# Attention outputs by features: values stationary on two column halves, probabilities moving and divided before they are transposed

## What is computed

```python
p_cmp = jnp.where(vis, jax.nn.softmax(s, axis=-1), 0.0)
o_cmp = jnp.einsum('bgrsc,bcgd->bsgrd', p_cmp.astype(vc.dtype), vc)
...
o = (g[:, :, 0] * o_cmp.astype(jnp.float32) + g[:, :, 1] * o_slc.astype(jnp.float32)
     + g[:, :, 2] * o_win.astype(jnp.float32))
...
m = jnp.maximum(jnp.max(s, axis=-1, keepdims=True), sk)
e = jnp.exp(s - m)
p = e / (jnp.sum(e, axis=-1, keepdims=True) + jnp.exp(sk - m))
o = jnp.einsum('bngrqk,bnkgd->bnqgrd', p.astype(vb.dtype), vb)
...
merged = jax.nn.sigmoid(ga) * (o_a @ w_branch_a[i]) + jax.nn.sigmoid(gb) * (o_b @ w_branch_b[i])
...
x = x + jnp.concatenate([o_a, o_b, o_c], axis=-1) @ w_out[l]
```

## Time and profile before

| | |
|---|---|
| device time, median of 3 runs | 1260.78 us (1260.34 to 1265.6) |
| device time of the profiled execution | 1260.99 us |
| its span | 1259.2 us |
| PE busy | 1228.6 us (98%) |
| DVE busy | 791.7 us (63%) |
| ACT busy | 609.6 us (48%) |
| GpSimd busy | 66.4 us (5%) |
| granted TensorE clock, mean | 0.997 |

### The profile page before, as it was taken

How to read it: one execution, slowest core, us unless ns; L and a number is a source line. 1 busy time by engine, 2 the same in 40 slices (tenths; PEclk the granted TensorE clock), 3 DMA queues, 4 the chain that set the end, 5 groups by cost and what they waited for, 6 DMA issues and landing times. The chain is left out here.

```text
span 1259.2 us, 21554 instructions
## 1 busy us (share of the span) xinstructions
PE 1228.6 (98%) x8764; PEld 1131.6 (90%) x8764; DVE 791.7 (63%) x1095; ACT 609.6 (48%) x831; POOL 66.4 (5%) x58
## 2 busy tenths in 40 slices
PE   8999999999999999999999899999999989999997
PEld 7999999989998999999999789999999978999996
DVE  4665556657866655555799655555458977654554
ACT  5444345355536443435755554444465464544343
POOL 0000000200000000000530000000004200000000
PEclk9999999999999999999999999999999999999999
DMA  9576565455335565556465056655644734566550
GB/s 286 176 227 193 175 184 149 129 159 169 134 119 199 179 192 197 173 193 185 151 126 168 28 174 203 197 175 193 187 140 119 159 101 151 174 195 192 176 198 33
DMA packets 200915, 209.62 MB, mean 166 GB/s; under 512 B 58136, under 2 KB 177552, under 8 KB 200848
## 3 DMA queue, kind: packets, MB, share of 16 engines
q1 hardware_dynamic: 200400, 208.21, 53.8%
q10 hardware_dynamic: 448, 0.46, 0.2%
HBM read 207.61 MB, written 1.05 MB: 166 GB/s over the span
## 5 line engine op out<-in xcount | busy, mean ns | idle before, releaser
L1366 DVE TENSOR_TENSOR w_lo<-raw,w_hi 128x2048 fp32r<-128x2048 f32 (+2 forms) x192 | 432.9, 2258 | 270.5 <-ACT w_hi L1014 269.9
L1014 ACT ACTIVATE w_hi<-raw 128x2048 fp32r<-128x2048 f32 (+2 forms) x192 | 359.4, 1876 | 246.3 <-PE bank L1890 214.8
L1890 PE MATMUL bank<-n_hi,w_hi 128*128 128x256 f32 (+1 forms) x1600 | 455.4, 285 | 1.5 <-DVE w_lo L1366 1.5
L1890 PE MATMUL bank<-n_hi,w_lo 128*128 128x256 f32 (+1 forms) x1600 | 452.8, 283 | 0.0
L1890 PE MATMUL bank<-n_lo,w_hi 128*128 128x256 f32 (+1 forms) x1600 | 452.7, 283 | 0.0
L1890 PEld LDWEIGHTS bank<-n_hi,w_hi 128*128 128x128 f32 (+1 forms) x1600 | 305.3, 191 | 5.6 <-DVE w_lo L1366 1.7
L1890 PEld LDWEIGHTS bank<-n_lo,w_hi 128*128 128x128 f32 (+1 forms) x1600 | 305.3, 191 | 2.1 <-issue 0.2
L1890 PEld LDWEIGHTS bank<-n_hi,w_lo 128*128 128x128 f32 (+1 forms) x1600 | 305.3, 191 | 0.0
L1890 PE MATMUL bank<-w_hi,hid_hi 128*128 128x512 f32 x440 | 172.7, 392 | 1.3 <-DVE hid_lo L1439 1.1
L1890 PE MATMUL bank<-w_lo,hid_hi 128*128 128x512 f32 x440 | 171.8, 391 | 0.0
L1890 PE MATMUL bank<-w_hi,hid_lo 128*128 128x512 f32 x440 | 171.4, 389 | 0.0
(11 more groups left out here) (268 smaller groups left out, 1485.5 us busy)
## 6 DMA issues: line engine op xcount, KB each, us to landing
raw<-in_w_ff_dram SPq DMA_DIRECT2D x64, 1024.0 KB, 5.3
raw<-in_w_in_dram SPq DMA_DIRECT2D x31, 1024.0 KB, 5.4
raw<-in_ffn_down_dram SPq DMA_DIRECT2D x22, 1024.0 KB, 4.9
raw<-in_ffn_up_dram SPq DMA_DIRECT2D x21, 1024.0 KB, 5.4
raw<-in_ffn_gate_dram SPq DMA_DIRECT2D x20, 1024.0 KB, 5.4
raw<-in_w_out_dram SPq DMA_DIRECT2D x12, 1024.0 KB, 5.1
raw<-in_w_in_dram SPq DMA_DIRECT2D x12, 256.0 KB, 4.0
raw<-in_w_uq_dram SPq DMA_DIRECT2D x24, 128.0 KB, 4.0
```

Source lines behind the costliest of these rows:

```text
L1014: nc.scalar.activation(wh(s)[:, c0:n], raw[:, s % RING, c0:n], ACT.Copy).then_inc(hi_ready, 1)
L1366: V.tensor_tensor(wl(s)[:, c0:n], raw[:, s % RING, c0:n], wh(s)[:, c0:n].bitcast(f32), ALU.subtract).then_inc(lo_ready, 1)
L1890: mm = MM(out, stat(k, a), mov(k, b), start=(first and k == 0 and n == 0), stop=(last and k == K - 1 and n == 2), skip_group_check=True)
```

## The change

Values become stationary, 64 columns of them, and the transposed probabilities move: the upper group writes partitions 0 to 63 of the output bank, the lower group 64 to 127, so that the output stands by features. Where heads share their values, one product takes all heads of a group (N = 256 or 512). The compressed, selected and window branches are summed in one bank (`output_of`), so the coefficients, sums and gates, have to be in the probabilities ahead. A new step `n` does that between `s` and `t`: DVE works out `pcoef`, GpSimd multiplies the upper group's probabilities with it, DVE the lower group's. The step `o` then only splits the bank into `on_hi` (ACT) and `on_lo` (DVE). The steps `ot` are gone, `mixt` transposes the retention's output alone, swa comes first in the first block, the branch product takes swa's weights first, and in the second block `wout` begins with its second half between the last rounds. `probsT` gets two more buffers.

```diff
-    S += gate[1] + [("cmp1", "v"), ("rope", 0, "kc")] + scores[3] + weighted[1] + turned[2]
+    S += gate[1] + [("cmp1", "v"), ("rope", 0, "kc")] + scores[3] + normed[2] + weighted[1] + turned[2]
...
-    S += gate[7] + [("sigmoid",)] + weighted[7] + turned[8] + [("ot", "a", 1), ("ot", "b", 0)] + weighted[8]
-    S += [("ot", "b", 1), ("branch",)]
+    S += gate[7] + [("sigmoid",)] + normed[8] + weighted[7] + turned[8] + [("cv", 1)] + weighted[8] + [("o", 0, "nsa", 1), ("branch",)]
...
+        scores, normed, turned, weighted = in_rounds(l, [("dsa", 0), ("dsa", 1), ("mla", 0), ("mla", 1)])
+        S += scores[0] + scores[1] + [("ukv", l)] + normed[0] + turned[0] + scores[2] + [("ukvv", l)] + normed[1] + turned[1]
+        S += [("rety", l)] + scores[3] + weighted[0] + normed[2] + weighted[1] + [("mixt", l)] + turned[2] + scores[4] + normed[3]
+        S += [("wout", l, 0)] + turned[3] + weighted[2] + normed[4] + turned[4] + weighted[3] + weighted[4]
+        S += [("wout", l, n) for n in range(1, 4)]
...
+                if st[0] == "n" and st[4] % 2 == 0:
...
+                    pool.wait_ge(coef_ready, CO[(l, a, t, next(r for r in rounds(a, t) if g in r))] + 1)
+                    by = pcoef[:, RSLOT[a], t, hs].unsqueeze(2).to_broadcast([P, nh, nk])
+                    p = probs[:, q % 4, 0:nh * nk].rearrange("p (h k) -> p h k", h=nh)
+                    nc.gpsimd.tensor_tensor(p, p, by, ALU.mult).then_inc(normed[0], 1)
...
+                elif kind == "n":
+                    _, l, a, t, g = st
+                    r = next(r for r in rounds(a, t) if g in r)
+                    if g != r[0]:
...
+                        dve.wait_ge(coef_ready, CO[(l, a, t, r)] + 1)
...
+                        V.tensor_tensor(p, p, bc(by, len(heads), nk), ALU.mult).then_inc(normed[1], 1)
+                        continue
+                    dve.wait_ge(exp_done, ATT[(l, a, t, r[1])] + 1)
...
+                    ins = V.reciprocal(c, sums)
+                    if a in GATE:
+                        link(ins)
+                        dve.wait_ge(*free_count(("toks", 0)))
+                        ins = V.tensor_tensor(c, c, of(gates[:, t, 8 * GATE[a]:8 * GATE[a] + 8]), ALU.mult)
+                    ins.then_inc(coef_ready, 1)
...
+                elif kind == "o":
+                    ob, ks, tok = output_blocks(st)
+                    act.wait_ge(pv_done, ON[st[1:]][1])
...
+                    nc.scalar.activation(on_hi[:, ks, tok], ob, ACT.Copy).then_inc(ot_hi, 1)
...
-                    pe.wait_ge(exp_done, q + 1)
+                    pe.wait_ge(normed[st[4] % 2], NRM[st[1:]] + 1)
...
-                    for i, h in enumerate(heads):
-                        for blk in range(t + 1):
-                            c = (i * (t + 1) + blk) * P
-                            mm = MM(acc[o % 2][:, h * HD:h * HD + HD], probsT[:, n % 2, c:c + P], values(a, h, blk),
-                                    start=(blk == 0), stop=(blk == t))
...
+                    for blk in range(t + 1):
+                        for i in range(nh if a == "mla" else 1):
+                            for rows_, heads, pT in sides:
+                                c0, n = column_of(a, heads[i]), (1 if a == "mla" else nh)
+                                mm = MM(ob[rows_, c0:c0 + n * P].rearrange("p (i c) -> p i c", c=P), values(a, heads[i], blk), pT[:, i:i + n, blk, :],
+                                        start=(first and blk == 0 and i == 0), stop=(blk == t), skip_group_check=True)
```

More of the change, by code:

```diff
@@ L128, in schedule @@
           ("rope", 0, "nq0"), ("proj", 0, "vv"), ("rope", 0, "sk"), ("proj", 0, "sq0"), ("rope", 0, "k"),
-          ("xpe", "k"), ("proj", 0, "nq1"), ("rope", 0, "sq0"), ("xpe", "v"), ("cmp1", "k")]
-    scores, turned, weighted = in_rounds(0, [("slc", 1), ("slc", 0)] + [(a, t) for a in ("win", "swa") for t in range(NT)])
+          ("xpe", "k"), ("proj", 0, "sq1"), ("rope", 0, "sq0"), ("xpe", "v"), ("cmp1", "k")]
+    scores, normed, turned, weighted = in_rounds(0, [("swa", 1), ("swa", 0)] + [(a, t) for a in ("slc", "win") for t in range(NT)])
@@ L168, in schedule @@
     return S
+GATE = {"cmp": 0, "slc": 1, "win": 2}
 HEADS = {"slc": 8, "win": 8, "swa": 8, "dsa": 4, "mla": 8}
@@ L201, in outputs @@
     def outputs(job):
[L202 to L218, removed]
+        return [("pv", l) + job] + ([("o", l) + job[:2]] if job[2] == last[job[:2]] and job[0] not in GATE else [])
+    return ([[("s", l) + job for job in jobs] for jobs in turns], [[("n", l) + job for job in jobs] for jobs in turns],
+            [[("t", l) + job for job in jobs] for jobs in turns], [[st for job in jobs for st in outputs(job)] for jobs in turns])
 PROJ = {(0, "kcvc"): [(512, 256)], (0, "misc"): [(1816, 128), (1280, 24)], (0, "kk"): [(768, 128), (1024, 128)],
@@ L420, in job @@
                 _small[0] += 1
-            if b is None and key[0] == "t":
+            if b is None and key[0] in ("t", "mixt"):
                 b = 2 + _turned[0] % 2
@@ L742, in values, with turned_probs, column_of, output_blocks @@
             return vm[:, blk, 64 * h:64 * h + 64]
+        def turned_probs(n):
+            return probsT[:, n % 4, :] if n % 4 < 2 else probsT2[:, n % 4 - 2, :]
+        def column_of(a, h):
+            return P * (h % 4 if a in ("slc", "win") else h // 2)
+        def output_blocks(st):
+            n = 2 if st[2] == "dsa" else 4
+            k0 = {"nsa": 0, "swa": 4, "dsa": 4, "mla": 0}[st[2]]
+            ob = acc[ON[st[1:]][0] % 2][:, 0:n * P].rearrange("p (k c) -> p k c", k=n)
+            return ob, slice(k0, k0 + n), slice(st[3] * P, st[3] * P + P)
         def mask_of(a, t):
@@ L751, in two_blocks @@
         RSLOT = {"slc": 0, "win": 1, "swa": 2, "cmp": 3, "mla": 4, "dsa": 5}
-        GATE = {"cmp": 0, "slc": 1, "win": 2}
         def quarter(q):
@@ L1335, in _ @@
                 elif kind == "wout" and st[2] < 2:
-                    ahead(SL[st])
+                    ahead(SL[st], 1 if st[1] and st[2] == 0 else 2)
         @block.vector
@@ L2223, in _ @@
                     _, l, a, t, g = st
-                    heads, n, o = groups(a, t)[g], PVN[st[1:]], ON[st[1:4]][0]
+                    r = next(r for r in rounds(a, t) if g in r)
+                    if g != r[0]:
+                        continue
+                    key = output_of(l, a, t)
+                    ob, begun = acc[ON[key][0] % 2], key in opened
                     if g == 0:
@@ L2353, in _ @@
                                 mm = MM(pb[:, :], (on if l else xn)(4 * half + k, a)[:, t * P:t * P + P], w(s, b)[:, k * 512:k * 512 + 512],
[L2354 removed]
+                                        start=(not last and k == 0 and j == 0), stop=(last and k == 3 and j == 2),
                                         skip_group_check=True)
[L2356 removed]
+                        if last and t == 0:
                             mm.then_inc(filled(("wq", l, 2 * c)), 1)
```

307 lines of the change are left out of this document (144 added, 163 removed).

## The result

The changed kernel takes 1302.61 us (median of four, 1298.91 to 1303.44). Beside four runs of the kernel before (median 1263.19, 1260.34 to 1265.88) that is a ratio of 1.031, 95% interval 1.027 to 1.034. The runs of the kernel before fall in two groups, 1258 to 1262 us at a mean granted clock of 0.995 to 0.998 and 1263 to 1269 at 0.990 to 0.995; its profile is of the first group, and every ratio here takes both. The prediction was 1300, range 1275 to 1320. The profiled execution took 1303.44 us with a span of 1301.6, where before had 1260.99 and 1259.2: the span is 42.4 us longer.

A forecast was written before the change was run, and what follows sets the result against it. PE, busy 98% of the span, was taken to bound the kernel. From 1261 us, 55.9 us of new waits come and 27.1 us of work and waits go (+28.8), and the clock adds 10: 1300 us, range 1275 to 1320.

The forecast's parts named there:

- The bound: Whole kernel: PE, busy 98% of the span, sets the end; PE work removed is won, PE waiting is lost.
- PE work that goes: On PE: value products 6.9 us less in the first block, 7.0 in both layers; transposes 4.4 less.
- Old waits: PE's waits in attention of layers 1 and 2, 7.3 us, and in the branch products, 1.46, go.
- the fast rival of 1234 us: Division ready when PE's value products end, so no new waits: 1234 us; chance 0.03.
- The chain of the wait: Ahead of each round's transposes PE waits for score step, coefficients, GpSimd's product and hops, less cover: 55.9 us in all.
- the first wait: First block, first round (swa, t=1): wait for the division with a rotation of 0.96 as cover, 3.8 us.
- The terms for the layers: Layers 1 and 2: four waits for the division in each, 2.9, 1.8, 4.3 and 3.8 us, sum 12.8.
- The lock: DVE and GpSimd share a port pair, locked for a whole instruction; GpSimd's product taken as 1.9 us, shortest 1.29.
- The clock: After some PE waits the clock halves, costing 1.65 us a stretch; six of 17 counted: +10 us, from 0 to 28.
- The rival in which every wait lowers the clock: All 17 waits on PE bring a low clock stretch: 28 us instead of 10, 1318 us; chance 0.12.
- The sum: Whole kernel: 55.9 us come and 27.1 go, +28.8, with +10 for the clock: 1300 us.
- The break-even of 1.6 us a wait: Mean new wait of PE, over 17 waits, at which the 27.1 us that go would be used up.

The follow-up runs named there:

- the last order: Changed kernel with divisions moved ahead on DVE and GpSimd, and output copies and splits moved later in first block and layers: 1247.16 us, ratio 0.988.
- the other orders: Nine experiments keeping the changed kernel's 8628 instructions: PE busy 1211.8 to 1213.5 us, median 1212.4, with their low clock taken off.
- the early order: Changed kernel with each division moved ahead in DVE's and GpSimd's order, no instruction added or taken away: 1257.56 us, ratio 0.994.
- the filled run: Changed kernel, order kept, with unused products of 256 columns put on PE ahead of each wait for the division: 1283.19 us, ratio 1.015.
- thin products: Changed kernel, order kept, with the division's products cut to the first key of each head: 1270.79 us, ratio 1.005.

## Why the prediction came out, step by step

- **The bound.** PE decides: right. DVE had 4 us more to do after the change and GpSimd 27, and neither is near the span in its total (61% and 7%); the time is PE's work plus PE's waits in every run.
- **PE work that goes.** Right for the value products. Where no wait hides it, in the last order above, a round of the first block with them takes 1.01 us from their start to the next (1.07 taken), where it took 1.84:

```profile
293.33 1.08 PE L2250 MATMUL bank<-probsT,scr 128*64 128x512 f32 x4
294.34 1.09 PE L2223 MATMUL bank<-cst,probs 128*128 128x128 f32 x8
```

  That is two products of 512 columns, one on each half, in little more than the 0.96 that one takes, and four of 256 take as long. Column halves do run side by side. The sum was over-sized: -16.8 against -18.3 by the table, -14.5 by the other orders. The place of what is missing can be read. PE's busy time in layer 1 and the stretch up to layer 2, before the change and in the last order (columns as above):

```profile
658.50:990.20 331.70, 324.96 (x2268) 297.18 (x2267) 213.96 (x301) 165.59 (x231) 22.40 (x17) 1.00 0.53 159
```
```profile
651.40:979.30 327.90, 321.45 (x2245) 291.55 (x2244) 215.44 (x306) 163.71 (x229) 29.48 (x22) 1.00 0.53 161
```

  It is 3.5 us less, and 3.6 from there to the end, where 3.5 + 1.3 = 4.8 was counted for each layer. The first block has some 8.2 of its 8.7. Which operation of the layers it is was not tested.
- **Old waits.** 8.8 us were booked as won, and this is a step that failed. The run without the division has PE idle for 1.3 us more than before, not 8.8 less. Under the new waits part of this didn't show: the table has 6.5 us less. It is why the fast rival of 1234 us could not be had by dropping the wait alone, and part of why the early order stopped at 1257.6.
- **The chain of the wait.** Right in its links and its place, in all 17 cases. It was over-sized: 43.7 for 55.9. GpSimd's product took 1.54 in all 15 whole-width cases where 1.9 was taken from the row beside a split; 15 x 0.36 = 5.4. The two hops to and from GpSimd took 0.05 each where 0.1 was taken, and the score step 1.39 for 1.46: some 0.17 a wait, 3 us. Of the rest, 1.1 is cover: the first wait was 2.24 for 3.8, also because the rotation that covers it ran at half the clock, 2.07 for 0.96 us. The terms for the layers were 12.8 and measured 9.5 in each; the remainder was not taken apart.
- **The lock.** The Trainium skill (SBUF — State Buffer, Who interferes with whom) has an exclusive lock for a DVE instruction with two inputs in SBUF beside a GpSimd one that reads SBUF. The rows of the early order agree with it: the small operation of DVE ended with GpSimd's, and the split, begun 0.98 us before GpSimd ended, took 0.85 us longer. For the pair of products no run can tell. DVE's, issued 0.05 us earlier, took 0.69 and GpSimd's 1.54. The 1.9 taken was a product of 1.29 blocked for 0.6; but the 1.27 to 1.29 are of the rotation's products, which have another second operand, and no run has the division's product without DVE's beside it. It may have been held up for 0.27 us, or for more, or not at all: 0.19 us for 2 columns, 0.85 for 256 and 1.54 for 512 also fit a length that goes by the columns alone.
- **The clock.** The step that failed most: 22.0 us for 10 by the windows, 19.4 by the filled run. The size of one stretch was right (3.5 us cost 1.7), but nine new ones came and not six, and several held for 7 us, at 2.5 to 3.1 each. The count had been taken from three waits before the change. The rival in which every wait lowers the clock gave 28 and was nearer, but its rule doesn't hold either: behind several of the 17 waits the clock stood at 1.00 (below).
- **The sum.** -12.2 in the waits and +12.0 in the clock cancel, which is luck. 1300 for 1302.6 is better than its terms; the range, which carried the ends of both, is what the argument supported. A slip without weight: the rounds that would gain by a full factor of two are 18, not 17.5.

The break-even of 1.6 us a wait was too high, with the clock or without it. With thin products the waits were 21.6 us, 1.3 for each of the 17 places, and that kernel was 0.5% slower than before, its span in the profile 10.0 us longer. Its low stretches cost 9.3 us more than before, so even at full clock 1.3 us a wait would only have been even: the old waits were not won, and the work saved was smaller.

## What to carry to other kernels

When a step is put between two others that were a round apart, ask what stands ahead of it in its engine's queue, and whether the waiting engine has only just released that; if so, the two run in step, and moving the new step up the queue by a whole slab can give the wait back (here 45 us of 1303, wait and clock together, with not one instruction changed). Price PE's waits at their length plus half of what PE does at the low clock behind them, here 0.4 to 0.5 us for each microsecond waited. And a wait taken away is won only when the list of waits of a run without it shows no other in its place.

## What the runs showed of the hardware that was not expected

- **Waits of one length, clocks of two levels.** The waits of 3.15 us at 753.36 and of 3.16 us at 1091.93, in the same place of two like layers, were followed by 0.51 for 7 us and by 1.00. Here they are, with the two of 1.80 us in the same layers, after which the first transposes are equally long, but the clock falls at 722 and holds at 1061:

```profile
721.11 0.66 PE L2221 MATMUL bank<-cst,probs 128*128 128x128 f32 x4 [1.80 <-POOL probs L994]
...
753.36 1.97 PE L2221 MATMUL bank<-cst,probs 128*128 128x128 f32 x8 [3.15 <-POOL probs L994]
...
1061.27 0.66 PE L2221 MATMUL bank<-cst,probs 128*128 128x128 f32 x4 [1.80 <-POOL probs L994]
...
1091.93 1.09 PE L2221 MATMUL bank<-cst,probs 128*128 128x128 f32 x8 [3.16 <-POOL probs L994]
```

  A single wait's effect on the clock can't be read off its length; what decides between the two was not found. In the profile of the filled run the wait of 3.2 us for the first rotation was followed by 1.00, where it was followed by 0.50 in the changed kernel.
- **Filling an idle PE with work that nobody uses** gave 19.4 us back, 1.5% of the run; PE still waited 11.2 us in 17 pieces of at most 1.5 us, and none of them lowered the clock.
- **GpSimd's product beside DVE's** took 1.54 us and DVE's 0.69, where the prediction had taken 1.9 for GpSimd's, while a small operation of DVE beside GpSimd's rotation waited for its end, 1.11 us for 0.16 in the early order and 0.89 in the one with swa's outputs moved.
